# Spreading seven modulation tiles over the q, k and v projections, and making the layer-2 rows of h half by half

## What is computed

```
def modulate(x, g, shift, scale):
    return rms_norm(x, g) * (1 + scale) + shift
...
        mod = (s_lat @ ada_w[layer] + ada_b[layer])[:, None, :]
        mod_c = s_ctx @ ada_w[layer] + ada_b[layer]
        sh1, sc1, g1, sh2, sc2, g2 = jnp.split(mod, N_MOD, axis=-1)
...
        h = modulate(x, norm1_g[layer], sh1, sc1)
        h_c = modulate(ctx, norm1_g[layer], csh1, csc1)
...
            q, k, v = qkv_heads(h, odd_w_qkv[i], odd_q_g[i], odd_k_g[i])
            q_c, k_c, v_c = qkv_heads(h_c, odd_w_qkv[i], odd_q_g[i], odd_k_g[i])
            y = _merge(neighbourhood_attention(q, k, v, k_c, v_c, odd_rpb[i])) @ odd_w_o[i]
```

## Time and profile before

| | |
|---|---|
| median of 3 runs | 2204.83 us (2202.77 to 2205.24) |
| the profiled execution, its own time | 2208.53 us |
| its span, first to last instruction | 2206.9 us |
| PE busy | 2081.7 us, 94% of the span |
| DVE, ACT, POOL busy | 845.5, 585.0, 72.1 us |
| second layer, q chunks 0 to 3 | about 594.7 to 606.8 us |
| q chunks 4 to 7; k; v | to 627.1; to 677.2; to 722.1 us |
| attention of the second layer | 722.1 to 801.0 us |

### The profile page before, as it was taken

How to read it: one execution, slowest core, us unless ns; L and a number is a source line. 1 busy time by engine, 2 the same in 40 slices (tenths; PEclk the granted TensorE clock), 3 DMA queues, 4 the chain that set the end, 5 groups by cost and what they waited for, 6 DMA issues and landing times.

```text
span 2206.9 us, 27387 instructions
## 1 busy us (share of the span) xinstructions
PE 2081.7 (94%) x11616; PEld 1393.6 (63%) x11616; DVE 845.5 (38%) x1566; ACT 585.0 (27%) x1002; POOL 72.1 (3%) x119
## 2 busy tenths in 40 slices
PE   7999999999999899999998999989899989999997
PEld 4777888778878579999988843433334333444332
DVE  4345443353575667755465521111211111111112
ACT  4223332342342655544366210000000000000001
POOL 0000000000000330000041000000000000000000
PEclk9999999999999999999999999999999999999999
DMA  9543343333431564545433899999999999999996
GB/s 368 196 153 115 115 152 115 112 108 105 153 115 47 211 210 161 176 161 200 169 119 149 329 364 395 428 427 428 429 427 428 427 427 428 428 427 427 427 410 281
DMA packets 164819, 592.88 MB, mean 269 GB/s; under 512 B 9138, under 2 KB 83890, under 8 KB 139348
## 3 DMA queue, kind: packets, MB, share of 16 engines
q1 hardware_dynamic: 163028, 589.68, 67.8%
q10 hardware_dynamic: 1664, 1.39, 0.2%
HBM read 590.00 MB, written 1.05 MB: 268 GB/s over the span
## 4 chain that ended last, share of the span: by engine, by line
PE 77%; DMA 14%; DVE 4%; ACT 3%; issue 2%; SPq 0%; ACTq 0%; DVEq 0%
PE ps L1008 23%; PE ps L290 14%; PE ps L291 14%; PE ps L292 13%; DMA ring<-in_w_up_dram 10%; PE ps L957 3%; PE ps L976 2%; DMA ring<-in_ada_w_dram 2%; DVE wr L1142 2%; PE ps L436 2%; ACT big L2128 1%; DMA ring<-in_even_w_in_dram 1%; PE ps L451 1%; PE ps L1033 1%; ACT wr L1827 1%
## 5 line engine op out<-in xcount | busy, mean ns | idle before, releaser
L1008 PE MATMUL ps<-ring,big 128*64 128x512 f32 x3008 | 679.9, 604 | 61.1 <-DMA ring<-in_w_up_dram 41.4
L1008 PEld LDWEIGHTS ps<-ring,big 128*64 128x64 f32 x3008 | 244.6, 139 | 466.5 <-issue 459.5
L290 PE MATMUL ps<-h_hi,wr 128*128 128x512 f32 (+1 forms) x960 | 338.5, 353 | 4.2 <-DVE h_lo L1295 2.6
L1142 DVE TENSOR_TENSOR wr<-ring,wr 128x1024 fp32r<-128x1024 f32 (+1 forms) x248 | 286.3, 1211 | 137.8 <-ACT wr L1827 137.7
L291 PE MATMUL ps<-h_lo,wr 128*128 128x512 f32 (+1 forms) x960 | 331.7, 346 | 0.0
L292 PE MATMUL ps<-h_hi,wr 128*128 128x512 f32 (+1 forms) x960 | 331.4, 345 | 0.0
L1827 ACT CAST wr<-ring 128x1024 fp32r<-128x1024 f32 (+1 forms) x248 | 239.3, 1032 | 117.1 <-PE ps L292 93.1
L290 PEld LDWEIGHTS ps<-h_hi,wr 128*128 128x128 f32 x960 | 183.5, 191 | 37.2 <-issue 11.5
L291 PEld LDWEIGHTS ps<-h_lo,wr 128*128 128x128 f32 x960 | 183.3, 191 | 22.3 <-issue 1.7
L292 PEld LDWEIGHTS ps<-h_hi,wr 128*128 128x128 f32 x960 | 183.3, 191 | 21.7
L2128 ACT ACTIVATE big<-ps,s 128x128 f32<-128x128 f32 x64 | 24.0, 456 | 364.0 <-PE ps L957 364.0
(11 more groups left out here) (343 smaller groups left out, 2630.7 us busy)
## 6 DMA issues: line engine op xcount, KB each, us to landing
ring<-in_w_gate_dram SPq DMA_DIRECT2D x62, 2048.0 KB, 22.1
ring<-in_w_up_dram SPq DMA_DIRECT2D x59, 2048.0 KB, 18.3
ring<-in_w_down_dram SPq DMA_DIRECT2D x57, 2048.0 KB, 22.1
ring<-in_ada_w_dram SPq DMA_DIRECT2D x24, 2048.0 KB, 10.9
ring<-in_ffn_w_up_dram SPq DMA_DIRECT2D x44, 1024.0 KB, 7.6
ring<-in_ffn_w_down_dram SPq DMA_DIRECT2D x16, 1408.0 KB, 6.2
ring<-in_w_in_dram SPq DMA_DIRECT2D x9, 2048.0 KB, 8.0
ring<-in_odd_w_qkv_dram SPq DMA_DIRECT2D x6, 2048.0 KB, 7.8
```

Of the source, the lines that this page charges most:

```text
L290: e.matmul(o, l[0], r[0], start=first, stop=False)
L1008: ins = e.matmul(pts[hf][HALF[z], :], lhs[:, k, HALF[z]], wt, start=k == 0, stop=False, skip_group_check=True)
L1142: e.tensor_tensor(wr[:, x], ring[:, x], h.bitcast(F32), SUB).then_inc(s_wlo, 1)
```

## The change

Three things are done together.

**Modulation tiles.** Tile 17 is read on PE after q chunk 5 (and `headsum(4)`), 18 after k chunk 9, 19 after k chunk 13, 20 after the second group of v. Each fold stands one chunk later, behind the next `headsum` (for v behind the third group). Tiles 21, 22 and 23 stay in the attention, in steps 3, 7 and 11. On ACT the copy of a tile stands behind the square of the next chunk and the root of the chunk itself.

**Rows of h.** `norm(2)` ends after the diagonals of the roots. `scale_half`, `lower_half` and ACT's `shift_half` make the latent half (i = 0) for all k first. The context half (i = 1) follows two chunks at a time, in iterations g = 0 to 3 of the loop over q chunks: on DVE ahead of the reciprocal of chunk g, on ACT (for g = 1 to 3) behind the root of chunk g - 1.

**Weight splits.** The four pieces of the second q tile (`W_QKV + 1`) are split between chunks of the latent half: on ACT behind k = 3 to 6, on DVE behind k = 4 to 7. The bank `rr` is held until g = 8.

```
+    MOD_QK = {5: 17, 9: 18, 13: 19}
+    MOD_NA = {3: 21, 7: 22, 11: 23}
...
         abreast([("qk", c) for c in range(4)], L, [(wpair(W_QKV), c) for c in range(4)],
-                lambda k: e.wait_ge(s_hlo, hz0[2] + 2 * k + 1), q=2, n=3)
+                lambda k: e.wait_ge(s_hlo, hz0[2] + k + 1), q=2, n=3)
...
             if g == 8:
                 e.wait_ge(s_hlo, hz0[3])
+                held.discard(full["rr", 2][0])
...
             rows(("qk", g), L if g < 8 else 512, t, g % 4)
             headsum(g - 1)
             wlast[t] = filled(("qk", g))
+            if g in MOD_QK:
+                mod_rows(MOD_QK[g])
+            if g - 1 in MOD_QK:
+                mod_fold(MOD_QK[g - 1])
...
+                if i == 0 and n == 1:
+                    mod_rows(20)
+                if i == 0 and n == 2:
+                    mod_fold(20)
...
-            if step % 2 and step < 14:
-                due = 17 + step // 2
+            if step in MOD_NA:
+                due = MOD_NA[step]
                 mod_rows(due)
...
+        def scale_half(k, i):
+
+            if i == k == 0:
+                e.wait_ge(*filled(("rr", 2)))
+            if k % 4 == 0:
+                e.wait_ge(*amul_at[1, 0, k // 4])
+            if k >= 3:
+                e.wait_ge(s_hlo, hz0[2] + KC * i + k - 2)
+            hs = slice(L * i, L * i + L)
+            e.scalar_tensor_tensor(wk[(0, 1, 3)[k % 3]][:, hs], xT[:, k, hs], amuls[1][:, 2 * k + i:2 * k + i + 1],
+                                   bank(("rr", 2))[:, hs], MULT, MULT).then_inc(s_hz, 1)
...
-        norm(2, add_mod(16))
+        norm(2, None)
...
+        scale_half(0, 0)
+        for k in range(KC):
+            if k < KC - 1:
+                scale_half(k + 1, 0)
+            lower_half(k, 0)
+            if k == 1:
+                mod_add(16)
+            if k >= 4:
+                lo(W_QKV + 1, k - 4, k - 3)
         for g in range(16):
-            if g % 4 == 0:
+            if g and g % 4 == 0:
                 lo(W_QKV + g // 4 + 1)
+            if g < 4:
+                for k in (2 * g, 2 * g + 1):
+                    scale_half(k, 1)
+                for k in (2 * g, 2 * g + 1):
+                    lower_half(k, 1)
...
+        def shift_half(i, k0=0, k1=KC):
+
+            for k in range(k0, k1):
+                hs = slice(L * i, L * i + L)
+                e.wait_ge(s_hz, hz0[2] + KC * i + k + 1)
...
+                if i == 0 and k >= 3 and k < KC - 1:
+                    hi(W_QKV + 1, k - 3, k - 2)
...
-        shift(2)
+        shift_half(0)
...
-        hi(W_QKV + 1)
-        e.wait_ge(s_hlo, hz0[3])
+        shift_half(1, 0, 2)
+        e.wait_ge(s_hlo, hz0[2] + KC)
         for g in range(16):
             if g and g % 4 == 0:
                 hi(W_QKV + g // 4 + 1)
             head_square(g)
             if g:
                 head_root(g - 1)
+            if g - 1 in MOD_QK:
+                mod_copy(MOD_QK[g - 1])
+            if 0 < g < 4:
+                shift_half(1, 2 * g, 2 * g + 2)
+                if g == 3:
+                    e.wait_ge(s_hlo, hz0[3])
```

More of the change, by code:

```diff
@@ L496, in abreast @@
                         ins.then_inc(fullsem(name))
-            if q is not None:
+            if q is not None and q != 2:
                 held.discard(full["rr", q][0])
@@ L1183, in norm @@
                 mod_add(0)
+            if q == 2:
+                return
             def scale(k):
@@ L1213, in norm, with lower_half @@
             e.tensor_copy(nrm[:, 9:10], nrm[:, 4:5]).then_inc(freesem(("rr", q)), 1)
+        def scale_half(k, i):
[8 more added lines that the diff above has]
+                                   bank(("rr", 2))[:, hs], MULT, MULT).then_inc(s_hz, 1)
+        def lower_half(k, i):
+            hs = slice(L * i, L * i + L)
+            e.wait_ge(s_hhi, hz0[2] + KC * i + k + 1)
+            e.scalar_tensor_tensor(hs_[1][:, k, hs], wk[(0, 1, 3)[k % 3]][:, hs], modcol(1, 0, k, i),
+                                   hs_[0][:, k, hs].bitcast(F32), ADD, SUB).then_inc(s_hlo, 1)
         def gated_add(name, c, l, part_, T):
@@ L1379, in dve @@
             e.scalar_tensor_tensor(dst, bank(("qk", g))[:, 0:n], gain, r, MULT, MULT).then_inc(freesem(("qk", g)), 1)
+            if g in MOD_QK:
+                mod_add(MOD_QK[g])
         lo(W_QKV + 5)
+        mod_add(20)
         for g in range(4):
@@ L1420, in dve @@
                 due = None
-            if step % 2 and step < 14:
-                due = 17 + step // 2
+            due = MOD_NA.get(step)
             if step in (2, 4, 6, 8):
@@ L1856, in shift @@
                                  bias=modcol(l, 3 * n, k, i)).then_inc(s_hhi, 1)
+        def shift_half(i, k0=0, k1=KC):
+            for k in range(k0, k1):
+                hs = slice(L * i, L * i + L)
+                e.wait_ge(s_hz, hz0[2] + KC * i + k + 1)
+                e.activation(hs_[0][:, k, hs], wk[(0, 1, 3)[k % 3]][:, hs], ACT.Identity,
+                             bias=modcol(1, 0, k, i)).then_inc(s_hhi, 1)
+                if i == 0 and k >= 3 and k < KC - 1:
+                    hi(W_QKV + 1, k - 3, k - 2)
         e.dma_start(cols[:, :], a["cols"]).then_inc(s_cols, 16)
@@ L1999, in act @@
                     head_root(15)
+                if i == 0 and n == 2:
+                    mod_copy(20)
         for step in range(20):
@@ L2017, in act @@
                     e.copy(turned_[u % 8], bank(("T", u))[:, :]).then_inc(freesem(("T", u)), 1)
-            if step % 2 and step < 14:
-                mod_copy(17 + step // 2)
+            if step in MOD_NA:
+                mod_copy(MOD_NA[step])
             if step in (2, 4, 6, 8):
@@ L2307, in sync @@
             w(W_QKV + i + 3)
-        for m in range(18, 24):
-            mod(m)
+            if i < 4:
+                mod(18 + i)
+        mod(22)
+        mod(23)
         w(W_O + 1)
```

2 lines of the change are left out of this document (added).

## The result

| | before | after |
|---|---|---|
| time, median (runs) | 2205.03 us (4) | 2225.00 us (4) |
| lowest to highest | 2202.77 to 2208.74 | 2221.19 to 2226.35 |
| the profiled execution | 2208.5 us | 2221.19 us |

The ratio is 1.0079, with a 95% interval of 1.0065 to 1.0093: 17.4 us slower (14.4 to 20.5). It is the ratio on record, not the quotient of the two medians, which lie 20.0 us apart; both lie in the interval. The forecast was 2218.5 us, +13.7, in a range of 2211 to 2225; the measured median stands at the upper end of that range.

What follows compares the result with a forecast made beforehand. PE was taken to lead the attention and bind k and v, with PE and DVE both full in q chunks 4 to 7. Terms: q +9.5, tiles +17.9, attention -13.6, sum +13.8; forecast 2204.8 + 13.7 = 2218.5 us, range 2211 to 2225.

Steps and rivals of the forecast that it cites:

- The signs listed ahead of the run: Expected in the profile: q chunk 4 near 612, two PE waits, k about 13.5 us later, folds waiting, attention near 65 us.
- The round trip: In q chunks 0 to 3: root, reciprocal, multiplication, scalings, shift and square chain to 4.4 us; q chunk 4 starts +0.7 us.
- PE's two waits for the multiplication: In q, PE waits for banks DVE frees: 2.0 us before chunk 5, and before head sum 4 +5.2 us over before.
- The folds of k: After tiles 18 and 19, each fold on PE waits 1.95 us for ACT's copy.
- The fold of q: After tile 17, the fold on PE waits 1.3 us for ACT's copy.
- a first low stretch: Behind the gap ahead of q chunk 4: PE's clock low for 3.5 us at 1.2 GHz, counted the same as before.
- the second stretch: Behind the gap before head sum 4 in q: clock down once more, 3.5 us at half speed, +1.6 us.
- The -13.6: Attention: four tiles leave and memory waits go, but DVE and ACT come up; -13.6 us, bounds -18.9 to -10.
- the rounds don't chain: Rival: q costs about 0 to 3 us, total +4 to +8, 2209 to 2213; less loss (+4 to +9) had chance 0.14.
- Faster: Rival: folds find copies ready, q costs 0, attention falls to PE's own work, -18.9; total -7.5, 2197; chance 0.05.
- Slower still: Rival: attention saves only 10 us and low clock stretches in q are longer; +19, 2224; chance 0.11.
- the two goals: Gains sought: 7.5 us of memory waits in the attention and some 4.6 us of gap before q chunk 4.

Runs made afterwards that it cites:

- the second execution: The whole change, unaltered, run once more against the kernel before: 1.0058, +12.8 us.
- rows part: Kernel before with only the rows of h in halves and the weight splits changed, all seven tiles left in the attention: 1.0043, +9.5 us.
- context at once: Rows of h and weight splits only, context half made in one go before q chunk 0, bank `rr` given back as before: 1.0005, +1.1 us against before.
- spread split: Rows of h and weight splits only, ACT's hi split of the third tile put in pieces behind roots 0 to 2: 1.0015, +3.3 us against before.
- two buffered traces: Kernel before with tiles 18, 20, 22 in a second buffer: 0.9969, -6.9 us; the same with tiles 18 to 23 read one step later: 0.9961, -8.6 us.
- tiles part alone: Kernel before with only the modulation tiles moved as in the change, rows of h as before: 1.0019, +4.2 us.

## Why the prediction was right, and where it was small

**The sign and the mechanism: right.** The signs listed ahead of the run are there, the first not by its letter: q chunk 4 was to start near 612, not near 608, and started at 607.88, in an execution that reached q 4.56 us earlier. Counted from the first matmul on h that is 17.73 us, where 17.4 was forecast (612.1 - 594.7); in the second execution, which reached q at 594.85, it started at 612.43. The round trip is 4.27 us where the rows summed to 4.4. PE's two waits for the multiplication are there, 1.56 and 5.59 us of idle time. A trace counts idle time from the modelled end of the matmul ahead, while in an unbroken stream the next one starts earlier; on the path they are a little longer. Chunk 5 would have started 0.24 behind head sum 3, at 612.19, and started at 614.10: 1.91 us (forecast 2.0). Head sum 4 came at 622.81 where it would have at 617.07: 5.74 (5.7). The folds of k came at 660.15, where PE would have gone on 0.46 behind its head sum of 657.73, as before (638.59 to 639.05): 1.96 (1.95). The fold of q came 1.54 late (632.16 against 630.38 + 0.24; forecast 1.3). The attention took 65.83 (65.3). From the first matmul on h to the start of k it took 15.2 us longer (17.73 + 29.87 against 16.72 + 15.67), where 13.65 was forecast (0.7 + 12.95).

**The term that was mis-sized: the low clock of PE, 1.0 to 1.8 us short in q and 1.2 in k.** The forecast counted a first low stretch as before, and one more, +1.6 (3.5 us at half speed are 1.7 rather). Three came. Windows of the kernel after, behind the wait of 5.59 and behind the wait of 1.19:

```profile
622.80:627.40 4.60, 4.59 (x18) 1.10 (x18) 4.60 (x5) 0.47 (x1) 0.00 (x0) 0.52 0.02 4
633.00:637.75 4.75, 4.75 (x29) 4.72 (x28) 0.89 (x3) 0.00 (x0) 0.00 (x0) 0.64 0.32 120
```

With PE busy, such a stretch loses what its clock lacks: 4.6 x 0.48 = 2.2 us and 4.75 x 0.36 = 1.7. The tile read in the first of them took 3.50 us, against the 1.92 of the earlier trace rows. The stretch in q chunk 4 was a little shorter than before (4.07 us from that chunk's start to head sum 3, against 4.57), -0.5. That makes +3.4 in place of +1.6. Taken from the other side, the stage's 14.2 less the waits and the tile's work, 1.91 + (5.74 - 0.4) + 2.85 + 1.54, leaves 2.6. So the term was between 1.0 and 1.8 too small. From the mean clock: of the 12.5 us at 1.2 GHz (0.21 x 29.87 / 0.5) only the 2.4 in the wait of 5.59 lie in PE's idle time, where they cost nothing; the other 10.1 lose half, 5.0 us, where 1.7 were lost before: +3.3. The Trainium skill (TensorE: Matmul & The Clock Gate, section "What's actually happening") calls the throttled state the default; the trace agrees at the second wait, with 0.52 over 622.80 to 627.40, and the sum that took the second stretch in was the better one.

In k the two tiles should have cost 9.6 and cost 10.8. The mean clock was 0.97 where it had been 1.00; 0.03 x 60.91 is 1.8 us, more than the 1.2 that are missing. It lies in one stretch, 661.3 to 664.8, behind the fold of tile 18: the chunk behind that fold took 7.61 us with its head sum, and the one behind the fold of tile 19 6.04, where the clock stayed at 1.00. With the folds one chunk later there is no wait in k, a clock of 1.00, and a length of 56.27 us. v came out 0.4 above its term.

**The attention: right, with a base that moves.** No wait for `ada_w` is left in the kernel after, and those that PE has are for DVE, as forecast:

```profile
PE ps L719 <- DVE at L1465: 5.0, 5, 2.7
```

Its pattern came as forecast: DVE's step 4 starts 14.37 us into the stage (14.4 forecast), step 10 at 40.02 (40.4), a pair of steps taking 8.55 (8.65). The end of that sum was loosely added: 762.5 + 5 x 3.15 + 1.5 is 779.75, and the 8.9 behind it is counted from PE's scores, while DVE's step 15 starts 1.3 us later (793.39); with 7.6 it comes to the 787.4 given. Not as forecast was the clock, counted as untouched: from 753.4, within a gap of 2.71 us that ended at 753.73, to 757.0 it was at 0.50, and the mean was 0.97. As DVE was in time all the same, its cost doesn't show apart.

The -13.6 stood against one execution of the kernel before, with 7.5 us of memory waits. In kernels with the same seven tiles in the same places, the attention took 79.8 (rows part), 81.3 (context at once) and 84.3 us (spread split), and its waits for `ada_w` were 8.2 to 9.5 us:

```profile
PE ps L439 <- DMA ring<-in_ada_w_dram: 9.5, 6, 3.0
```

So 78.9 was a short sample; in the 81.3 and the 84.3 a lower clock (0.98 and 0.96, PE busy 1.6 and 3.3 us longer) has its part too. That would explain why taking the wait away brought 6.9 and 8.6 us in the timed runs, while the attention's length fell only by 3.5 and 3.8 against that one trace; this is inferred from lengths of single executions, not measured over many. It fits that in ten of the eleven traces of versions other than before the stages from q to the end of the attention, taken against that one trace, come out longer than the timed difference says; the mean of all eleven is 3.0 us. For the whole change it is 0.1 in the first trace and 4.7 in the second, hence the luck above. In the two buffered traces themselves the memory wait fell by 4.9 and 7.5 us, while PE was busy 1.3 and 1.6 us longer, at a clock of 0.98, and in the second waited 2.3 us more for DVE.

**The rivals.** That the rounds don't chain falls by the roots 4.27 us apart. Faster falls with it. "Slower still" (+19, 2224) is close to the measured 2225.0, but its mechanism is only half there: the longer low stretches in q are, the attention at its lower bound of -10 isn't (it fell by 13.1), though PE's clock did fall in it once.

**The question that was not asked** is what the two goals were worth. The gap ahead of q chunk 4 was 4.6 us, and no version closed it: with the context half at once 3.5 us of waits stand there in place of 3.2. The waits in the attention were 7.5, and they can be had for less: with a second buffer and nothing moved the kernel is 6.9 us faster.

## What to carry to other kernels

Work that is woven between the steps of several in-order engines can tie rounds together that were independent, even where each engine looks half idle: here a round then took 4.27 us, against 3.4 of PE's work on a chunk. Sum one full round before weaving, and compare it with what the leading engine does in that time. Where a wait comes from one buffer being read and filled in turn, give it a second buffer before moving work into stages that are full, since moved work is paid again in full (11.2 us of 11.4 here). And put what reads another engine's copy one step later than the order of the code suggests: here four copies hidden were worth 6 us.

## What was not expected of the hardware

- A wait of 1.19 us was followed by a low stretch of PE's clock in q: at 1.00 over 631.00 to 633.00, then 0.64 in the mean from 633.00 to 637.75 with PE busy throughout. In the attention before, with gaps to 3.3 us, it had stayed at 1.00; in the one after it fell at a gap of 2.71. In k the same wait of 1.40 us was followed by a low stretch at tile 18 and by none at tile 19, and with the tiles part alone it was the other way round (low from 683.9 to 687.5, behind tile 19's fold). What tells them apart is open.
- The length of the first low stretch in q varies from execution to execution, at code that is the same up to there: it lasted 3.5 us in the kernel after (606.7 to 610.2) and 7.0 in the rows part (609.1 to 616.1). q chunk 4 took 4.07 us in the kernel after (607.88 to 611.95) and 5.41 in the rows part (610.71 to 616.12), behind waits of 4.12 and 4.13.
- Idle matmuls in the waits brought the clock from 0.79 to 0.94 and from 0.93 to 1.00, and the time of the kernel didn't follow in either case. In the second, DVE was the limit of the stage; for the first the cause is open.
